# The even mixing part of a hybrid decoder step: tiles of 128 tokens mixed as one chunk, or as two chunks of 64, and the output projection's pieces in other places of the step

## The reference, cut to what matters

```python
def rwkv7_recurrence(r, log_decay, k, v, kk, a, S0):
    def step(S, inp):
        r_t, lw_t, k_t, v_t, kk_t, a_t = inp
        s_kk = jnp.einsum('bhvk,bhk->bhv', S, kk_t)
        S = (S * jnp.exp(lw_t)[:, :, None, :] - s_kk[..., None] * (kk_t * a_t)[:, :, None, :]
             + v_t[..., None] * k_t[:, :, None, :])
        return S, jnp.einsum('bhvk,bhk->bhv', S, r_t)
    ...
y, s_rwkv_new = rwkv7_recurrence(r, log_decay, kr, vr, kk, a, s_rwkv)
y = head_groupnorm(y, RWKV_GN_EPS) * ln_w + ln_b
y = y + jnp.sum(r * kr * r_k, -1, keepdims=True) * vr
o_rwkv = y.reshape(B, L, RWKV_W) * jax.nn.silu(gb)
out = jnp.concatenate([o_ret, o_rwkv], axis=-1) @ w_out
```

## Time and profile before

| | us |
|---|---|
| median of three runs | 3101.29 |
| the profiled execution | 3103.8 |
| its span, first to last instruction | 3101.8 |
| TensorE busy in the span | 2999.8 |
| VectorE busy | 1930.9 |
| ScalarE busy | 1003.0 |
| GpSimd busy | 503.7 |
| even mixing, first to last instruction | 716.8 to 1567.4 |

### The profile page before, as it was taken

The page is one execution under the profiler, slowest core; times in us unless marked ns, Lnnn a source line. Parts: engine busy times, 40 slices in busy tenths (PEclk is TensorE's granted clock), DMA queues, the critical chain, the costliest instruction groups (busy, mean ns, idle before and its releaser), DMA issues. The chain is left out here.

```text
span 3101.8 us, 89481 instructions
## 1 busy us (share of the span) xinstructions
PE 2999.8 (97%) x38740; PEld 2724.6 (88%) x38740; DVE 1930.9 (62%) x4060; ACT 1003.0 (32%) x2220; POOL 503.7 (16%) x519
## 2 busy tenths in 40 slices
PE   9999999996999999999989999999997999999998
PEld 8999999996888887888789999999995688888886
DVE  5212344445777777777445156776765688888886
ACT  5211210003343343343167122222223344444441
POOL 0000000001333333343300000000001111111112
PEclk9999999998999999999899999999998999999999
DMA  8421221215233433433353221221214223333333
GB/s 260 120 87 60 74 75 63 67 50 175 73 109 114 121 115 106 121 120 108 108 197 115 67 71 61 77 78 60 77 50 156 77 84 99 97 100 97 96 104 130
DMA packets 227704, 311.69 MB, mean 100 GB/s; under 512 B 34793, under 2 KB 166129, under 8 KB 227185
## 3 DMA queue, kind: packets, MB, share of 16 engines
q1 hardware_dynamic: 213840, 260.30, 26.4%
q0 software_dynamic: 9152, 29.94, 3.3%
q10 hardware_dynamic: 4320, 15.73, 1.8%
HBM read 210.18 MB, written 95.72 MB: 99 GB/s over the span
## 5 line engine op out<-in xcount | busy, mean ns | idle before, releaser
L414 DVE SCALAR_TENSOR_TENSOR po_stage<-po_work,po_cw,po_stage 128x424 f32<-128x424 f32 (+1 forms) x360 | 232.1, 645 | 28.3 <-issue 1.7
L595 PE MATMUL po_ps<-po_xnT_hi,po_w_hi 128*128 128x424 f32 x960 | 205.0, 355 | 0.0
L595 PE MATMUL po_ps<-po_xnT_hi,po_w_lo 128*128 128x424 f32 x960 | 204.4, 355 | 0.0
L595 PE MATMUL po_ps<-po_xnT_lo,po_w_hi 128*128 128x424 f32 x960 | 204.1, 354 | 0.0
L299 ACT ACTIVATE po_work<-po_ps 128x424 f32<-128x424 f32 (+1 forms) x120 | 61.7, 514 | 407.9 <-PE po_ps L595 407.9
L595 PEld LDWEIGHTS po_ps<-po_xnT_hi,po_w_hi 128*128 128x128 f32 x960 | 180.2, 188 | 5.2
L595 PEld LDWEIGHTS po_ps<-po_xnT_hi,po_w_lo 128*128 128x128 f32 x960 | 180.4, 188 | 4.5
L595 PEld LDWEIGHTS po_ps<-po_xnT_lo,po_w_hi 128*128 128x128 f32 x960 | 180.2, 188 | 4.6
L595 PE MATMUL pe_ps<-pe_w_hi,pe_xnT_hi 128*128 128x256 f32 x1088 | 153.8, 284 | 5.5 <-ACT pe_xnT_hi L299 5.2
L595 PE MATMUL pe_ps<-pe_w_lo,pe_xnT_hi 128*128 128x256 f32 x1088 | 153.5, 284 | 0.0
L595 PE MATMUL pe_ps<-pe_w_hi,pe_xnT_lo 128*128 128x256 f32 x1088 | 153.3, 284 | 0.0
(11 more groups left out here) (463 smaller groups left out, 7140.4 us busy)
## 6 DMA issues: line engine op xcount, KB each, us to landing
me_ring<-scratch_w_lo SPq DMA_DIRECT2D x68, 512.0 KB, 3.9
mo_c<-scratch_ch_o SPq DMA_DIRECT2D x51, 512.0 KB, 3.7
scratch_ch_o<-po_stage SPq DMA_DIRECT2D x96, 212.0 KB, 1.9
scratch_tok_e<-pe_stage SPq DMA_DIRECT2D x136, 128.0 KB, 1.9
pe_raw<-in_w_in_e POOLq DMA_DIRECT2D x52, 256.0 KB, 4.3
me_xs<-scratch_ch_e SPq DMA_DIRECT2D x17, 768.0 KB, 6.8
po_raw<-in_w_in_o POOLq DMA_DIRECT2D x48, 256.0 KB, 4.0
scratch_ch_e<-pe_stage SPq DMA_DIRECT2D x52, 212.0 KB, 1.9
```

Source lines behind the costliest of these rows:

```text
L414: return nc.vector.scalar_tensor_tensor(out=o, in0=a, scalar=s, in1=b, op0=op0, op1=op1)
L595: last = nc.tensor.matmul(out, left.bitcast(F32R), right.bitcast(F32R), start=(i == 0 and k == 0), stop=(i == 2 and k == KD - 1))
```

## The change

The tile stays 128 tokens, but the RWKV heads are mixed in two chunks of 64 (CK = 64). Decays restart at each chunk; key and query products are made only within a chunk, on 64*64 quarters of the array, for each half of a head pair and each chunk; G2T (queries against the low factors) now comes from the same products as IL and is kept for two tiles. The level of block 64 falls away with its tile TB, its mask and its copies, and the diagonal copies become two masked multiplications. The right side, the solve and the state update are done once for each chunk, the second chunk after the first one's state; the part of outputs and right side that depends on values is made for both chunks together (`values_part`). ScalarE copies the right side and, in two halves, the outputs, which VectorE then centres from SBUF. On ScalarE the tangent for the low-rank input stands after the turned queries and keys, and the outputs of retention are copied after the turned mixed rows. On TensorE the projection's pieces 0 to 5 stand singly at six places and 6 and 7 together before `turn_mix`; the retention outputs stand after it. On VectorE the low products stand ahead of the inverse roots and the mixed rows. GpSimd makes the factors of the state's decay per chunk. In the host's layout the tables shrink to 64 columns and four masks are added. Of the diff, the functions that make the products and passes (some removed lines and all of the step lists are left out; the lists follow as rows):

```diff
 LEVELS = [1 << j for j in range(7)]
+CK = 64
...
+            def from_state(t, c):
+                at, over = rows_of(c), rows_of(1 - c)
+                await_chunk(pe, "state_new", t - 1 + c, 1 - c)
+                for b in range(4):
+                    cols = slice(b * P, (b + 1) * P)
+                    if t == PT:
+                        l, r = (KST[:, b, 0, :], KST[:, b, 1, :]), ident
+                    else:
+                        l, r = (KR[t % 2][:, 0, b, at], KR[t % 2][:, 1, b, at]), s_wk[:, b].rearrange("p h v -> p (h v)")
+                    last_op = mm(A_[at, cols], l[0], r, start=False, stop=b == 3)
+                    mm(C_[over, cols], l[1], r, start=False, stop=False)
+                last_op.then_inc(E["rhs_ready"], 1)
...
+            def values_part(t):
                 if t == PT:
                     sample_state_products(t)
                 await_(pe, "o_copied", t)
                 await_(pe, "mixT_written0", t - 1)
+                if t == 0:
+                    await_(pe, "low_read", 1)
+                await_(pe, "mg_read", t)
+                await_(pe, "tok_written", t)
                 for h in range(H):
+                    cols = slice(h * WN, (h + 1) * WN)
+                    for w, bank in enumerate((A_, C_)):
+                        for c in range(2):
+                            at = rows_of(c)
+                            mm(bank[rows_of(c ^ w), cols], MG[at, h, w, :], tokV[t % 2][at, h, :], start=h == 0, stop=t == PT and c == 1 and h == H - 1)
+            def solve(t, c):
+                at = rows_of(c)
+                if c == 0:
+                    pe.wait_ge(s_ptc, LV[t + 1])
+                    await_(pe, "diagonals_copied", t)
+                    await_(pe, "ret_state_new", min(t, PT - 1))
+                await_chunk(pe, "rhs_copied", t, c)
+                for h in range(H):
+                    last_op = mm(B_[at, h * WN:(h + 1) * WN], TF[at, h, :], rhs[at, h, :])
                 last_op.then_inc(E["u_ready"], 1)
+            def state_of_chunk(t, c):
+                at = rows_of(c)
+                if c == 0:
+                    await_(pe, "mixT_written1", t - 1)
+                for left, right in ((tokK, tokV[t % 2]), (tokB, wv)):
+                    if left is tokB:
+                        await_chunk(pe, "wv_ready", t, c)
+                    for b in range(4):
+                        for half in range(2):
+                            p0 = 64 * half
+                            last_op = mm(D_[p0:p0 + 64, b * WN:(b + 1) * WN], left[t % 2][at, b, p0:p0 + 64], right[at, 2 * b + half, :],
+                                         start=left is tokK and b == 0, stop=left is tokB and b == 3)
+                            if left is tokB and b == 3:
+                                last_op.then_inc(E[f"delta{half}_ready"], 1)
             def outputs_of_solved(t):
+                await_chunk(pe, "wv_ready", t, chunks_of(t)[-1])
                 for h in range(H):
+                    for c in chunks_of(t):
+                        at = rows_of(c)
+                        last_op = mm(C_[rows_of(1 - c), h * WN:(h + 1) * WN], G2T[at, t % 2, h, :], wv[at, h, :], start=False, stop=h == H - 1)
                 last_op.then_inc(E["y_ready"], 1)
...
+            def with_own_chunk(n, which, banks, event):
                 for b in range(4):
                     for k, bank in enumerate(banks):
                         p0 = 64 * k
-                        last_op = mm(bank[:, b * P:(b + 1) * P], BK[p0:p0 + 64, 0, b, :], KR[n % 2][p0:p0 + 64, b, which, :])
+                        for c in range(2):
+                            at = rows_of(c)
+                            last_op = mm(bank[at, b * P:(b + 1) * P], BK[p0:p0 + 64, which, b, at], KR[n % 2][p0:p0 + 64, :, b, at])
                         if b == 3:
                             last_op.then_inc(E[f"{event}{k}_ready"], 1)
...
             def low_products(m):
                 for k, bank in enumerate((C_, D_)):
                     await_(dve, f"keys{k}_ready", m)
-                    last_op = tt(IL[:, k:H:2, :], heads(bank, P), bc(n2[m % 3][:, k:H:2], P), M)
+                    both = heads(bank, P)
+                    tt(IL[:, k:H:2, :], both[:, :, 0:CK], bc(n2[m % 3][:, k:H:2], CK), M)
+                    last_op = tt(G2T[:, m % 2, k:H:2, :], both[:, :, CK:P], bc1(T("incl", m), 4), M)
                 last_op.then_inc(E["low_read"], 1)
                 dve.drain()
-                mask = blocks[:, 7 if m == PT else 6, :]
-                for k in range(4):
-                    at = slice(k * Q, (k + 1) * Q)
-                    tt(ILc[at], IL[at, :, at], bc1(mask[at], H), M)
-                dve.drain()
-                tt(ILc[:], ILc[:], bc1(blocks[:, 5, :], H), AD)
+                j = 10 if m == PT else 8
+                tt(XA[:], IL[:, :, Q:2 * Q], bc1(blocks[:, j + 1, :], H), M)
+                tt(ILc[:], IL[:, :, 0:Q], bc1(blocks[:, j, :], H), M)
+                dve.drain()
+                tt(XA[:], XA[:], bc1(blocks[:, 5, :], H), AD)
+                dve.drain()
+                tt(ILc[:], ILc[:], XA[:], AD)
...
+            def solved(t, c):
+                at = rows_of(c)
+                await_chunk(dve, "u_ready", t, c)
+                tt(wv[at], heads(B_, WN)[at], bc(n2[t % 3][at], WN), M).then_inc(E["wv_ready"], 1)
+            def new_state(t, c):
                 for half in range(2):
                     s = s_wk[64 * half:64 * half + 64, :, half, :]
```

More of the change, by code:

```diff
@@ L675, in even_block_tables @@
     low = [((t[:, None] // seg == t[None, :] // seg) & (t[:, None] < t[None, :])).astype(np.float32) for seg in (P, DEC_T)]
-    return np.concatenate([block_tables()] + [np.tile(m, (P // Q, 1)) for m in low], 1)
+    side = [np.repeat(np.arange(P // Q) % 2 == k, Q)[:, None].astype(np.float32) for k in range(2)]
+    return np.concatenate([block_tables()] + [np.tile(m, (P // Q, 1)) for m in low] + [np.tile(m, (P // Q, 1)) * k for m in low + [np.ones((Q, Q))] for k in side], 1).astype(np.float32)
 def pair_table():
@@ L886, in level_count, with turn_count @@
             return LV[n] + levels_of(n).index(b) + 1 if b in levels_of(n) else None
+        def turn_count(n, b):
+            return sum(len([c for c in levels_of(i) if c < Q]) for i in range(n)) + levels_of(n).index(b) + 1
         def await_(eng, name, n):
@@ L1604, in _ @@
                 if t is not None:
-                    solved(t)
+                    solved(t, 0)
+                if m is not None:
+                    raw_keys(m)
+                if n == 0:
+                    split_weights(3)
+                if t is not None and t < PT:
+                    new_state(t, 0)
                 if n is not None:
+                    turn_blocks(n, 2)
                     mask(n, 4)
+                if n == 0:
+                    split_weights(4)
+                    split_weights(5)
                 if m is not None:
@@ L1610, in _ @@
                 if t is not None and t < PT:
-                    new_state(t)
-                if n == 0:
-                    split_weights(4)
-                    split_weights(5)
+                    solved(t, 1)
                 if n is not None:
                     turn_blocks(n, 4)
+                    mask(n, 8)
+                if n == 0:
+                    split_weights(6)
+                    split_weights(7)
+                if m == 1:
+                    dve.wait_ge(s_wl[3], 16)
+                if m is not None:
+                    factors(m)
+                if t is not None and t < PT:
+                    new_state(t, 1)
+                if n is not None:
+                    masked(n)
                 if t is not None:
@@ L2023, in _, with beside @@
                 last_step = p == PT
-                if t is not None:
-                    right_side(t)
-                if n == 0:
-                    keep_clock(8)
+                def beside(count, *parts):
+                    if p is not None and not last_step:
+                        for part in parts:
+                            project(p, part)
+                    elif p is None and n is not None:
+                        keep_clock(count)
                 if n is not None:
```

557 lines of the change are left out of this document (219 added, 338 removed).

## The result

The changed kernel took 3168.8 us (median of 4 runs, 3153.2 to 3180.5) against 3103.8 for the kernel before on the same chip (4 runs): ratio 1.0208, 95% interval 1.0154 to 1.0262. The forecast was 3051. Its profiled execution took 3171.6 us, 67.8 more than the one of before. The even mixing part grew by 61 us (908.1 against 846.9, from VectorE's first instruction in it to its last). What follows it grew by 7.8, to 1542.6, where the prediction had allowed 3; in the fifteen profiles of this study, where its code is the same, it lies between 1527 and 1545 in no order, so only the 61 need a cause.

What follows compares the result with a forecast made beforehand. TensorE, saturated in the even mixing part, was the bound: 6.0 us less list minus 3.1 waits, 2.9 a step, 44 over 15 steps, plus 6 at the ends: 50 off 3103.8, median 2.5 lower, 3051 (range 3030 to 3072).

Steps and rivals of the forecast that it cites:

- The list: TensorE's work laid end to end in a steady step: 16.98 us leaves, 10.96 comes, 6.0 less a step.
- B: Row tiles writing one PSUM bank exclude each other on TensorE; 2.14 of the 6.0 goes, 3073 us; chance 0.12.
- C: Four 64*64 quarters of TensorE's array run only two at a time; 6.0 becomes 2.8, about 3079 us; chance 0.10.
- The first wait: End of step: TensorE waits 1.7 us for the mixed rows, a 7.8 chain against 6.1 of work beside it.
- The second and third wait: TensorE waits 0.3 us for the first chunk's state and 0.6 for masked key products before the factors' transposition.
- Waits 3.1; bounds 1 and 6: Sum of four late hand-offs to TensorE in a step: 3.1 us, between 1 and 6.
- The clock should stay at 1.00 within the steps: TensorE's granted clock in the steady steps was expected to remain at 1.00.
- Rival E: Slower: VectorE's chain from key scores to mixed rows takes over, wait 5.7, waits sum 7.1, some 3125 us; chance 0.05.
- The prediction's own sign that it was too fast: If the clock falls in steady steps where it did not before, the forecast is too fast.
- SP's queue is passed by nothing new: On SP, only two ring loads for the next step are asked for at the step's end, three pieces before use.

Runs made afterwards that it cites:

- the wait filled: Changed kernel with ten idle identity products on TensorE while it waits for the mixed rows at a step's end: 3140.7 us, ratio 1.0120.
- the dense one: Kernel before the change with the first product group of levels 2 and 4 issued three times over, adding 256 small instructions a step: 3268.0 us, ratio 1.0518.

## Why the prediction was wrong

**The list** was predicted to shrink by 6.0 us a step and shrank by 44.39 - 37.65 = 6.74. Values 1.09 (1.07 predicted), solve 1.07. Four quarters run side by side, and upper and lower row tiles write one bank at that price, so rivals B and C are out; the trace disagrees with the rule that B rested on (the Trainium skill, TensorEngine Tiling (Array Packing), Restrictions and Gotchas).

**The first wait**, for the mixed rows: mechanism right, 2.9 instead of 1.7. The chain from the low products on took 8.9 us instead of 7.8. The three passes to the mixed rows take 4.4 us from the first start to the last end, where I had taken 2.99 from the earlier trace rows (VectorE first, then GpSimd at the same time):

```profile
1266.32 1.57 DVE L1374 TENSOR_TENSOR me_yw<-me_yw,me_st 128x512 f32<-128x512 f32 x1
1267.97 1.62 DVE L1374 TENSOR_TENSOR me_yw<-me_yw,me_g 128x512 f32<-128x512 f32 x1
1269.67 1.05 DVE L1374 TENSOR_TENSOR me_mix<-me_yw,me_Bt 128x512 f32<-128x512 f32 x1
1266.31 1.04 POOL L1052 TENSOR_TENSOR me_osb<-me_osb,me_st 128x512 f32<-128x512 f32 x1 [5.28 <-DVE me_st L1546]
1267.49 1.55 POOL L1052 TENSOR_TENSOR me_mix<-me_osb,me_g 128x512 f32<-128x512 f32 x1
1269.01 1.16 POOL L1052 TENSOR_TENSOR me_qsT<-me_qkT,me_tab_p 128x256 f32<-128x256 f32 x1
```

Before, only the first of the three (1.42) ran beside a pass of GpSimd, until 1145.57; the two behind it took half as long:

```profile
1146.19 0.69 DVE L1333 TENSOR_TENSOR me_yw<-me_yw,me_g 128x512 f32<-128x512 f32 x1
1146.95 0.69 DVE L1333 TENSOR_TENSOR me_mix<-me_yw,me_Bt 128x512 f32<-128x512 f32 x1
```

So the 2.99 was the price of one pass beside GpSimd and two without; now GpSimd works beside all three, beside the last for half of its length. That this is what makes them slow is read from these rows alone; no run varied it.

**The second and third wait** (state 0.3, masks 0.6) hardly came: 0.1 together. (The third was also mis-added: its passes sum to 5.7, not 6.0.)

**The step that failed** is "Waits 3.1; bounds 1 and 6" together with "The clock should stay at 1.00 within the steps". The waits are 6.96: 2.9 for the mixed rows and 3.9 unnamed, of which 3.5 fetching. I priced products by array time alone, and 64*64 products on four quarters bring 128 entries in 1.09 us, beside level groups with 128 in 0.7. The list that I shortened was also what gave the instruction packets their time. The clock adds 3.8. Sum: -6.7 + 6.5 + 3.8 = +3.5 a step, 49 us over 14 steps; the part's 61 has the rest in its first and last steps. Rival E had the condition (waits over 6.0) and the sign, but another mechanism: its chain was to bring a wait of 5.7, and brought 2.9; with VectorE's order undone the kernel was still not faster than before. The prediction's own sign that it was too fast, a clock that falls in the steady steps, is what came.

**SP.** "SP's queue is passed by nothing new" was true and beside the point: all of the step's transfers but the four ring loads are asked for in its first 10 us (DMA share 0.5 to 0.7 in its first 18 us, 0.01 in the 7 us that follow), and that is where the change packed the small products.

## What to carry to other kernels

Before making products smaller or denser, count queue entries (product and weight load each one) per microsecond of every stretch, not over the whole step: here 22 of the 30 blocks of 256 that passed in under 3 us ended in a wait for instructions, and blocks of up to 6.8 us did where the packet came late, mostly while data loads ran. Spread large products between the small groups, and keep load bursts out of dense stretches. A pause in the middle of a group, without a releaser and a multiple of 256 entries from the last (semaphore entries counted), is this; one at a group's start can be a data wait that the profile doesn't name.

## What was not expected of the hardware

Pauses of 0.9 to 4 us on TensorE were followed by 3.4 us or more at 1.2 GHz in nearly every step (not always: see the wait filled), 4.0 us a step lost where the waits themselves were 7.0. How long it stayed low differs: up to 10.2 us in the changed kernel, up to 13.7 us in the dense one, but only 3.4 us behind two of the dense one's longest pauses; what decides it isn't shown. And the end of the pause is late in a regular way: 1.24 to 1.67 us from the packet's end to the first instruction, in all 34.
